# Small matrix products grouped by their rows of the array, and an earlier output projection, in a two-block recurrent network kernel

## The reference, cut to what matters

```python
# block 1
proj = rms_norm(x, norm_mix_w) @ w_in                 # 3072 columns: xa, ga, qb, fb, ib, gb
ya = rg_lru(conv(xa), ...) * silu(ga)                 # 512 channels, a gated recurrence
yb = hgrn2_branch(qb, fb, ib, gb, ...)                # 4 heads of 128, chunks of 64 tokens
h  = x + concat([ya, yb]) @ w_out                     # "out1"
gate = sigmoid(rms_norm(h, ple_norm_w) @ w_ple_gate + b)
h  = rms_norm(h + gate * (p @ w_ple_proj), final_norm_w)
# block 2
mod = silu(c) @ ada_w + ada_b                         # a 1024 x 6144 product for one vector
h  = rms_norm(x, pre1_w) * (1 + sc1) + sh1
y_gla = gla_attention(...)   # 4 heads, keys of 64, values of 128, chunks of 64
y_ml  = mlstm_memory(...)    # 4 heads, keys of 64, values of 128
y_s5  = s5_ssm(...)          # 32 groups of 16 channels, 64 complex states each
merged = gates0*(y_gla @ proj_gla) + gates1*(y_ml @ proj_ml) + gates2*(y_s5 @ proj_s5)
x = x + (1 + gt1) * rms_norm(merged @ w_out, post1_w)
x = x + (1 + gt2) * rms_norm(swiglu_ffn(...), post2_w)
```

## Time and profile before

| | us |
|---|---|
| median of 3 runs (lowest, highest) | 2403.74 (2397.98, 2403.79) |
| the profiled execution | 2396.57 |
| its span, first to last instruction | 2394.8 |
| PE busy | 2307.3 (96%) |
| DVE, ACT, POOL busy | 1042.5, 625.3, 1151.5 |

### The profile page before, as it was taken

How to read it: one execution, slowest core, us unless ns; L and a number is a source line. 1 busy time by engine, 2 the same in 40 slices (tenths; PEclk the granted TensorE clock), 3 DMA queues, 4 the chain that set the end, 5 groups by cost and what they waited for, 6 DMA issues and landing times.

```text
span 2394.8 us, 29286 instructions
## 1 busy us (share of the span) xinstructions
PE 2307.3 (96%) x11096; PEld 1858.7 (78%) x11096; DVE 1042.5 (44%) x1188; ACT 625.3 (26%) x719; POOL 1151.5 (48%) x1106
## 2 busy tenths in 40 slices
PE   5999996999999999999999999999999999999997
PEld 3778885777777878777788878877888888888885
DVE  6777655345642251171367334726623200323306
ACT  5454332244523131121123232224311000111111
POOL 2443230666551323231375233466666676666675
PEclk8999998999999999999999999999999999999998
DMA  4223333222241111111111234342433333333343
GB/s 177 80 80 124 131 123 132 91 84 84 95 148 36 54 45 53 54 45 61 44 54 44 78 107 141 123 158 88 167 96 96 97 105 101 96 97 97 117 151 122
DMA packets 68758, 231.92 MB, mean 97 GB/s; under 512 B 7344, under 2 KB 8512, under 8 KB 68672
## 3 DMA queue, kind: packets, MB, share of 16 engines
q1 hardware_dynamic: 65216, 218.15, 27.3%
q10 hardware_dynamic: 3456, 12.58, 1.3%
HBM read 205.54 MB, written 25.17 MB: 96 GB/s over the span
## 4 chain that ended last, share of the span: by engine, by line
PE 84%; DVE 5%; issue 4%; ACT 3%; POOL 1%; DVEq 1%; DMA 1%; SPq 1%; POOLq 1%; ACTq 1%
PE PG L575 39%; PE PG L659 16%; PE PG L612 13%; PE PG L1036 5%; PE PX L764 1%; POOL WL L495 1%; PE PX L1001 1%; PE PX L760 1%; DVE PX L1692 1%; PE PG L1048 1%; PE PX L999 1%; PE PX L771 1%; POOLq L494 1%; PE PX L921 0%; PE PX L918 0%
## 5 line engine op out<-in xcount | busy, mean ns | idle before, releaser
L495 POOL TENSOR_TENSOR WL<-WRAW,WH 128x1024 fp32r<-128x1024 f32 (+2 forms) x304 | 700.3, 2304 | 45.1 <-issue 0.9
L492 POOL TENSOR_TENSOR TOUCH<-TOUCH 128x2 f32<-128x2 f32 x304 | 89.9, 296 | 1162.9 <-PE PG L659 407.7
L575 PE MATMUL PG<-UL,WH 128*128 128x512 f32 x1120 | 436.5, 390 | 0.0
L575 PE MATMUL PG<-UH,WH 128*128 128x512 f32 x1008 | 396.3, 393 | 6.1 <-POOL WL L495 3.6
L575 PE MATMUL PG<-UH,WL 128*128 128x512 f32 x1008 | 392.8, 390 | 0.0
L493 POOL TENSOR_SCALAR WH<-WRAW 128x1024 fp32r<-128x1024 f32 (+2 forms) x304 | 312.4, 1028 | 0.0
L575 PEld LDWEIGHTS PG<-UL,WH 128*128 128x128 f32 x1120 | 210.7, 188 | 45.2 <-issue 1.9
L575 PEld LDWEIGHTS PG<-UH,WH 128*128 128x128 f32 x1008 | 189.5, 188 | 50.5 <-issue 7.2
L659 PE MATMUL PG<-UH,WH 128*128 128x512 f32 x544 | 225.8, 415 | 0.0
L575 PEld LDWEIGHTS PG<-UH,WL 128*128 128x128 f32 x1008 | 189.7, 188 | 39.8
L659 PE MATMUL PG<-UL,WH 128*128 128x512 f32 x544 | 215.3, 396 | 0.0
(11 more groups left out here) (479 smaller groups left out, 3556.9 us busy)
## 6 DMA issues: line engine op xcount, KB each, us to landing
WRAW<-up_w SPq DMA_DIRECT2D x88, 512.0 KB, 3.5
ADA<-ada_w SPq DMA_DIRECT2D x24, 1024.0 KB, 5.8
WRAW<-down_w SPq DMA_DIRECT2D x48, 512.0 KB, 3.6
WRAW<-out_w SPq DMA_DIRECT2D x30, 512.0 KB, 3.5
WRAW<-zg_w SPq DMA_DIRECT2D x24, 512.0 KB, 3.5
gates<-STG ACTq DMA_DIRECT2D x24, 512.0 KB, 2.6
WK<-gates SPq DMA_DIRECT2D x24, 512.0 KB, 3.4
WRAW<-gla_w SPq DMA_DIRECT2D x18, 512.0 KB, 3.5
```

What stands on the lines that cost most here:

```text
L492: pool.tensor_tensor(TOUCH[:, 0:2], TOUCH[:, 2:4], TOUCH[:, 4:6], ALU.add)
L495: pool.tensor_tensor(WL[:, r, 0:n], WRAW[:, r, 0:n], WH[:, r, 0:n].bitcast(F32), ALU.subtract).then_inc(w_split, 1)
L575: mm = pe.matmul(PG[:, bank, :], w[:, r, P * k:P * k + P], v, start=first and k == 0 and n == 0, stop=last and k == kbs - 1 and n == 2)
```

## The change

**Order of small products.** In `la_core`, the scores of the two heads are issued in turns for each chunk; the numerator is issued by half of the tokens, first the four products of 128 rows, then the eight over the head's rows, with one opening flag a bank. The mLSTM numerator likewise. In `s5_block` the eight products of 128 rows are issued together and before the wait on `s5["x"]`, and then the sixteen of 64 rows, upper and lower rows in turns; the products at L982 alternate between the two halves of the output rows.

**ya in its own place.** YAH and YAL (blocks 46 to 53, where the ada ring, STG and TMP lie) take the parts of blocks 0 to 3. ACT makes them in the last hgrn2 head right behind `la_exps`, before it empties slot 0; DVE makes the low parts behind `keys`, before it empties slot 1. For that all 24 ada products are done in the first three heads (7, 7 and 6), none in the last. The last head's filler takes tile 0 two blocks ahead and has a quarter already behind the transposes.

**Order of stages.** `ple_w` now comes between `out1a` and `out1b`, its input goes to UH and UL, the first half's sum of squares is put behind its fifth tile, and the second half's behind the first two gate tiles. The products with `glu_w` now wait for each tile's split when that tile comes.

```diff
-                for u in range(5):
-                    ada_pair(7 + 5 * i + u)
+                for u in range(7 + 7 * i, min(14 + 7 * i, 3 * KB)):
+                    ada_pair(u)
...
-            def products_by_block(t, kbs, xh, xl, ready, count, u):
-                blocks = list(range(kbs))
+            def products_by_block(t, kbs, x_at, ready, count, u, first_tile_ahead=0):
+                a = first_tile_ahead
+                parts = [(k, r) for r in range(2) for k in range(a)] + [(k, r) for k in range(a, kbs) for r in range(2)]
...
-                for hh in range(nh):
-                    rows = slice(dk * hh, dk * hh + dk)
-                    for t in range(TT):
-                        for c in range(2):
-                            at = P * t + CH * c
+                for t in range(TT):
+                    for c in range(2):
+                        at = P * t + CH * c
+                        for hh in range(nh):
+                            rows = slice(dk * hh, dk * hh + dk)
...
-                    for t in range(TT):
-                        if t == TT // 2:
-                            filler()
-                        o = PX[:, t // 4, P * (t % 4):P * (t % 4) + P]
-                        pe.matmul(o, WK[:, vt[hh], P * t:P * t + P], WK[:, att[hh], P * t:P * t + P],
-                                  start=True, stop=False)
-                        for c in range(2):
...
+                    for half in range(2):
+                        if half:
+                            filler()
+                        for t in range(4 * half, 4 * half + 4):
+                            pe.matmul(PX[:, half, P * (t % 4):P * (t % 4) + P], WK[:, vt[hh], P * t:P * t + P],
+                                      WK[:, att[hh], P * t:P * t + P], start=t % 4 == 0, stop=False)
+                        for n in range(8 * half, 8 * half + 8):
+                            at = CH * (n % 8)
+                            mm = pe.matmul(PX[:, half, at:at + CH], states[:, P * n:P * n + P],
+                                           WK[rows, qe0, CH * n:CH * n + CH], start=False, stop=n % 8 == 7)
...
-                        (0, 2, 2, 1, 0, 1, 2) if last else (2, 0, 2, 2, 0, 1, 1))
+                        (1, 0, 2, 1, 0, 1, 3) if last else (2, 0, 2, 2, 0, 1, 1))
...
+            pe.wait_ge(ple_ready, 2)
+            for n in range(8):
+                U = UNIT0["ple_w"] + n
+                pe.wait_ge(slot_free[U % 2], U // 2)
+                product(TILE0["ple_w"] + n, n % 2, U % 2, 2, UH, UL)
+                if n == 4:
+                    half_sum(OUT1_ACC, post_acc, 3)
...
+                for g in range(8):
+                    pe.matmul(PX[:, 2 + g % 2, P * (g // 2):P * (g // 2) + P], WK[:, 6, P * g:P * g + P],
+                              WK[:, 3, P * g:P * g + P], start=g < 2, stop=False)
                 pe.wait_ge(s5["x"], i + 1)
+                for ri in range(2):
+                    for g in range(8):
+                        rows, at = slice(64 * (g % 2), 64 * (g % 2) + 64), P * (g // 2)
+                        mm = pe.matmul(PX[:, 2 + g % 2, at:at + P], WK[rows, 8, 512 * ri + at:512 * ri + at + P],
+                                       WK[rows, 2, 512 * ri + at:512 * ri + at + P], start=False, stop=ri == 1 and g >= 6)
...
+                if last:
+                    act.wait_ge(ada_done, 3 * KB)
+                    for j in range(4):
+                        act.activation(YAH[:, j, :], H[:, j, :], ACT.Copy).then_inc(sp_hi, 1)
...
+                if last:
+                    for j in range(4):
+                        out1_low(j)
```

More of the change, by code:

```diff
@@ L62 @@
 STREAM = [
-    ("rg_w", 8, (8, 8)), ("hg_w", 16, (8, 8)), ("out1_w", 2, (8, 8)), ("out1a", 6, (8, 8)), ("out1b", 6, (8, 8)),
-    ("ple_w", 8, (2, 2)), ("gatea", 8, (8, 8)), ("gateb", 8, (8, 8)), ("misca", 2, (4, 4)), ("gla0a", 6, (8, 8)),
+    ("rg_w", 8, (8, 8)), ("hg_w", 16, (8, 8)), ("out1_w", 2, (8, 8)), ("out1a", 6, (8, 8)), ("ple_w", 8, (2, 2)),
+    ("out1b", 6, (8, 8)), ("gatea", 8, (8, 8)), ("gateb", 8, (8, 8)), ("misca", 2, (4, 4)), ("gla0a", 6, (8, 8)),
     ("miscb", 2, (4, 4)), ("gla0b", 6, (8, 8)), ("zg0", 2, (8, 8)),
@@ L83 @@
 UNIT0, N_UNITS = columns([
-    ("rg_w", 8), ("hg_w", 16), ("out1_w", 2), ("out1a", 3), ("out1b", 3), ("ple_w", 8), ("gatea", 4),
+    ("rg_w", 8), ("hg_w", 16), ("out1_w", 2), ("out1a", 3), ("ple_w", 8), ("out1b", 3), ("gatea", 4),
     ("gateb", 4), ("misca", 1), ("gla0a", 3), ("miscb", 1), ("gla0b", 3), ("zg0", 2), ("gla1", 6), ("zg1", 2), ("ml0", 6), ("zg2", 4), ("ml1", 6), ("zg3", 4), ("s5_w", 4), ("zg4", 8),
@@ L615, in product @@
                 mm.then_inc(tile_done, 1)
[L617 to L620 removed]
+            def products_by_block(t, kbs, x_at, ready, count, u, first_tile_ahead=0):
+                a = first_tile_ahead
+                parts = [(k, r) for r in range(2) for k in range(a)] + [(k, r) for k in range(a, kbs) for r in range(2)]
                 def run(n_blocks):
[L623 to L629, removed]
[L630 to L638 removed]
+                    for _ in range(2 * n_blocks):
+                        k, r = parts.pop(0)
+                        if k == 0:
+                            pe.wait_ge(w_split, t + r + 1)
+                            if u:
+                                pe.wait_ge(slot_free[r], u)
+                        pe.wait_ge(ready, count + k + 1)
+                        xh, xl = x_at(k)
+                        for half in range(2):
+                            tok = slice(512 * half, 512 * half + 512)
+                            for n, (w, x) in enumerate(((WH, xh), (WH, xl), (WL, xh))):
+                                mm = pe.matmul(PG[:, 2 * r + half, :], w[:, r, P * k:P * k + P], x[:, tok],
+                                               start=k == 0 and n == 0, stop=k == kbs - 1 and n == 2)
+                        if k == kbs - 1:
+                            mm.then_inc(tile_done, 1)
                 return run
@@ L793, in _ @@
             for u in range(3):
-                for g in half_unit("out1a", u, 0):
+                for g in half_unit("out1a", u, 0, out1_half):
                     pass
-            for u in range(3):
-                for g in half_unit("out1b", u, 1):
-                    if (u, g) == (0, 1):
-                        half_sum(OUT1_ACC, post_acc, 3)
-            pe.wait_ge(ple_ready, 2)
-            with pe.Fori(0, 4) as i:
-                for n in range(2):
-                    pe.wait_ge(slot_free[n], UNIT0["ple_w"] // 2 + i)
-                    product(TILE0["ple_w"] + i * 2 + n, n, n, 2, PH, PL)
-            half_sum(OUT1_ACC, post_acc, 6)
+            pe.wait_ge(ple_ready, 2)
[5 more added lines that the diff above has]
+                    half_sum(OUT1_ACC, post_acc, 3)
+            for u in range(3):
+                for g in half_unit("out1b", u, 1, out1_half):
+                    pass
             pe.wait_ge(norm_lo, 24)
@@ L1291, in _ @@
                 act.wait_ge(p_loaded[j], 16)
-                act.activation(PH[:, j, :], WK[:, 19 - j, :], ACT.Copy).then_inc(ple_hi, 1)
+                act.activation(UH[:, j, :], WK[:, 5 + j, :], ACT.Copy).then_inc(ple_hi, 1)
             def out1_square(h, u):
-                U = UNIT0["out1a"] + 3 * h + u - 1
+                U = UNIT0["out1b" if h else "out1a"] + u - 1
                 for s in range(2):
@@ L1888, in hg_head @@
                 la_gaps(hg, 1, 0, 7, WK[:, 0, :])
-                ada(4 + 5 * i)
+                if not last:
+                    ada(4 + 7 * i)
                 dve.wait_ge(hg["exps"], i + 1)
```

148 lines of the change are left out of this document (75 added, 73 removed).

## The result

The changed kernel takes 2343.79 us (median of 4 runs, 2340.46 to 2346.89), the kernel before 2401.26 beside it: a ratio of 0.9764 (0.9746 to 0.9783). Five more runs of the changed kernel in a later set gave 2337.95 (2337.54 to 2345.22), ratio 0.9751 (0.9735 to 0.9767); the median of all nine is 2342.05. The forecast was 2342. The profiled run took 2344.27 with a span of 2342.5: 52.3 us less than before, where the sum had said 57.7.

A forecast was written before the change was run, and what follows sets the result against it. PE, busy 96% of the span, was taken as the bound; 23.7 + 1.1 + 8.0 + 0.8 + 7.8 + 14.5 + 0.5 + 1.3 = 57.7 us off 2394.8, plus 1.8 and 3, gave 2342 us, range 2331 to 2364.

The forecast's parts named there:

- Last head, 23.7: Last hgrn2 head: PE's waits for DVE's low parts shrink and `out1a` starts earlier, 23.7 us saved, ends 19 and 25.
- Rival 3: Last hgrn2 head: DVE leads, with slow low parts and late hand-overs, losing 5 to 10 us of 23.7; 2349, chance 0.14.
- The ada products, 0: First three hgrn2 heads: the added ada products on DVE, 2.3 us each, fit into its idle time and cost 0.
- Small products: GLA, mLSTM and S5: grouping by row height removes steps of 0.33 to 0.39 us; 8.0, 7.8 and 18.0 us.
- The order of stages, -1.1: From `out1a` to the gates: the second half's sum of squares no longer makes PE wait, 1.1 us saved.
- mLSTM, 7.8: mLSTM numerator: 7 changes of row height per head become 2, 0.39 us each there and back, 7.8 us saved.
- GLA, 8.8: GLA stage: 8.0 us from grouping the numerator's products by row height, 0.8 from the scores in turns.
- S5, 14.5: S5 readout: 18.0 us saved by grouping and turns over four blocks, less 3.5 of new waits for DVE.
- the wait of 2.9: S5 block 0: PE asks 4.5 us earlier, DVE has only 1.59 idle before the output, so PE waits 2.9.
- rival 4: S5: waits drop TensorE to 1.2 GHz; if held through 384 filler matmuls it costs 77 us, 2419; chance 0.03.
- `glu_w`, 1.3: Start of `glu_w`: the first part of tile 0's split is done during the 2.5 us wait, 1.3 us saved.
- the 3 added to it: Final forecast: 3 us added because the three runs' median lay 7.2 above the profiled execution and the lowest 1.4.

## Why the prediction was right, and where it was not

- **Last head, 23.7: right** (23.66). The start of `out1a` is 1.1 later than forecast (398.56, not 397.4) because the whole trace is 1.1 later ahead of the heads; that start varies from 187.2 to 189.0 between profiles. PE waits once for DVE's low parts, 3.09 instead of 17.9 in four waits; 3.2 was forecast. Rival 3 is out. 6.3 of the 23.7 are PE's own time for the same products, which ran in part at the low level before (11.9 withheld, much of it inside the waits; 1.7 now).
- **The ada products, 0: right.** The three heads before the last take 168.45 to 168.47 in every profile.
- **Small products: right to 0.1** in all three kinds of numerator and readout, by the starts of the earlier trace rows. What I had cost at 0.33 and 0.39 for there and back is what each removed change gave back.
- **The order of stages, -1.1: wrong, it is +1.7.** I credited the wait of 1.1 for a sum of squares to the sum ahead of the gates. In both traces it stands behind them (586.66 before, 565.82 after), at a product that the change doesn't touch. And I took the wait before `out1b` for one that had merely moved. Before, none stood ahead of the gates, where two ones-products lay between the short tiles and the first gate tile; the 1.24 is new, because a full split now follows a short tile with nothing between. The kernel with the late ones-product, which puts them there again, took 1.45 back. The kernel before:

```profile
511.01 1.02 PE L566 MATMUL PX<-WK,ONES 128*128 128x512 f32 x2
511.87 1.02 PE L567 MATMUL PX<-WK,ONES 128*128 128x512 f32 x2
512.71 0.47 PE L575 MATMUL PG<-UH,WH 128*128 128x512 f32 x1
...
586.66 1.12 PE L566 MATMUL PX<-WK,ONES 128*128 128x512 f32 x2 [1.06 <-DVE WK L1686]
```

- **mLSTM, 7.8: the step is right, its yield was not seen in the first profile.** The groups gave 7.77. The clock took 8.5 more than before in that run (15.4 and 6.8 withheld) and nothing more in the second (6.8; stage 260.12, 7.75 less than before). Over six profiles the stage is only 2.7 shorter than over three with the old order. The failing step is the assumption behind the sum, that PE's level falls only behind waits: it also falls in the quiet stretch of 4-row, mask and 64-row products, with PE busy. The kernel before had it too, in two of four heads, in rows that I didn't read. Whether the grouping makes these falls more frequent stays open.
- **GLA, 8.8: right** (8.02 and 0.8); the other 3.2 of the 12.0 go with the low level, 3.4 before and none after.
- **S5, 14.5: the wait of 2.9 was forecast in block 0 and came in four of the eleven profiles with S5's new order** (2.6 each), not in the first. I had read one slow copy ahead of block 0's output in the earlier trace rows as DVE's pace (2.60 from 1228.78 on, beside POOL's split; 0.42 in the two blocks behind it); without it DVE would have been idle there for 3.8 (1.59 and the copy's 2.2), nearly as long as the 4.15 of the others, and the wait forecast there would have been under 1. What decides from run to run whether the copy meets the split stays open. Where the wait came, a fall of the clock behind it (1.7 withheld in each of the four) cost about 1 more (block 1 at 34.94 to 35.16 and not 34.2). That is rival 4's mechanism, at a hundredth of its price. Rival 4 had argued that in the last head the clock was back within 4 us of work each time; behind the third and the fourth of the waits on L1880 it took 4.4 and 4.8.
- **`glu_w`, 1.3: 2.8.** The wait fell from 2.55 to 1.04, 1.5, as worked out, and with it went the low level behind it, 1.3, which I hadn't counted: from S5's last output product to the ninth product of `glu_w` PE took 53.07 before and 50.25 after. (The table cuts at the first such product, ahead of the wait that is left.) Before, then after:

```profile
1395.86 0.77 PE L635 MATMUL PG<-GH,WH 128*128 128x512 f32 x1 [2.55 <-POOL WL L495]
1396.42 0.63 PE L635 MATMUL PG<-GLO,WH 128*128 128x512 f32 x1
...
1345.86 0.50 PE L644 MATMUL PG<-GH,WH 128*128 128x512 f32 x1 [1.04 <-POOL WL L501]
1346.19 0.39 PE L644 MATMUL PG<-GLO,WH 128*128 128x512 f32 x1
```

That the median came within 2 us of 2342 is in part luck. The errors ran both ways: 8 in mLSTM and 2.8 in the order of stages and 1.1 at the start against 3.2 in GLA, 2.3 in S5 and 1.4 in `glu_w`. And the 5.4 by which the sum was too large was covered in part by the 3 added to it.

The Trainium skill, page TensorE: Matmul & The Clock Gate (Part 3), has loads overlap with running matmuls only when the row group differs. The group without turns speaks against it in this kernel: its 32 records, 16 in one half and then 16 in the other, take 0.107 each, no more than the 0.112 of the rows that the forecast goes by. The turns bring that down to 0.062.

## What to carry to other kernels

Read the starts of small matmuls, not their durations: a change of row height costs 0.33 to 0.40 there and back, and grouping by height takes it away as often as it stood there (8.02 us in GLA and 7.77 in mLSTM, against 8.0 and 7.8 worked out). For two row heights in one bank group that is arithmetic and can be forecast to a tenth. Then profile twice: a stage with several microseconds of quiet products can come out 8 us apart in two runs of one program, and a single profile credits or blames the wrong edit for it. The shorter group is certain, the shorter stage is not: in mLSTM the clock took back some of the gain in most profiles.

## What the hardware showed beyond that

- TensorE's granted clock fell to the 1.2 GHz level while PE was busy without a gap, in or right behind stretches of 4-row and mask products (3.3 us) and 64-row scores (2.0), and the mean granted clock went from 0.53 in one window of 6 us to 1.00 in the next, of dense work. Which heads it struck changed from run to run.
- A VectorE copy of 128x508 elements took 0.40 to 0.43 us in 49 cases and 2.60 in the six in which it lay beside GpSimd's split of a weight tile (2.64), and ended 0.3 after the split. The copy of 128x1024 ahead of it took 0.69 with GpSimd idle and 1.42 to 1.44 in the same six.
- 64-row products with upper and lower rows in turns run at 0.062 us a record (1.98 for 32), those through one half and then the other at 0.107 (3.43).
